# Where the weight buffers, the activation rows and the inner rows begin within 256 bytes

## Time and profile before

| | |
|---|---|
| median of 3 runs | 2599.0 us |
| span of the profiled execution | 2597.1 us |
| TensorE matmuls busy | 99% of the span, 16140 matmuls |
| VectorE busy | 61% |
| ScalarE busy | 46% |
| HBM | 180 GB/s over the span |

### The profile page before, as it was taken

How to read it: one execution, slowest core, us unless ns; L and a number is a source line. 1 busy time by engine, 2 the same in 40 slices (tenths; PEclk the granted TensorE clock), 3 DMA queues, 4 the chain that set the end, 5 groups by cost and what they waited for, 6 DMA issues and landing times.

```text
span 2597.1 us, 41960 instructions
## 1 busy us (share of the span) xinstructions
PE 2574.5 (99%) x16140; PEld 2308.9 (89%) x16140; DVE 1574.0 (61%) x2195; ACT 1188.0 (46%) x1603; POOL 26.8 (1%) x68
## 2 busy tenths in 40 slices
PE   9999999999999999999999999999999999999998
PEld 8999888888888888898999999988999988888886
DVE  5544856556556555565565566666866676666655
ACT  5543445444444344443444454445544444444442
POOL 1000000000000000000000000000000000000000
PEclk9999999999999999999999999999999999999999
DMA  7564555656565666574455566555576656777653
GB/s 250 178 178 130 162 181 178 197 189 194 194 185 184 198 180 194 177 219 140 131 172 169 163 195 191 179 198 163 158 194 177 184 178 196 195 182 188 194 186 122
DMA packets 467827, 468.76 MB, mean 180 GB/s; under 512 B 9294, under 2 KB 384190, under 8 KB 466910
## 3 DMA queue, kind: packets, MB, share of 16 engines
q1 hardware_dynamic: 465648, 459.31, 58.0%
q0 software_dynamic: 2064, 7.82, 0.9%
HBM read 464.93 MB, written 2.10 MB: 180 GB/s over the span
## 4 chain that ended last, share of the span: by engine, by line
PE 93%; DVE 4%; ACT 1%; DMA 1%; issue 1%; SPq 0%; DVEq 0%; ACTq 0%
PE ps L674 16%; PE ps L677 11%; PE ps L678 11%; PE ps L679 11%; PE ps L706 10%; PE ps L708 10%; PE ps L707 10%; PE ps L675 8%; DVE w_lo L2048 1%; DMA raw<-in_w_kv_mem 1%; PE ps L1077 1%; PE ps L1106 0%; PE ps L767 0%; ACT w_hi L1413 0%; PE ps L1113 0%
## 5 line engine op out<-in xcount | busy, mean ns | idle before, releaser
L2048 DVE TENSOR_TENSOR w_lo<-raw,w_hi 128x1024 fp32r<-128x1024 f32 (+1 forms) x876 | 1049.8, 1209 | 784.5 <-ACT w_hi L1413 782.5
L1413 ACT ACTIVATE w_hi<-raw 128x1024 fp32r<-128x1024 f32 (+1 forms) x876 | 904.5, 1045 | 923.1 <-PE ps L708 416.7
L677 PE MATMUL ps<-xa,w_hi 128*128 128x256 f32 (+2 forms) x2304 | 658.9, 286 | 2.0 <-DVE w_lo L2048 2.0
L679 PE MATMUL ps<-xa,w_lo 128*128 128x256 f32 (+2 forms) x2304 | 650.2, 282 | 0.0
L678 PE MATMUL ps<-xa,w_hi 128*128 128x256 f32 (+2 forms) x2304 | 649.8, 282 | 0.0
L674 PE MATMUL ps<-xa,w_hi 128*128 128x512 f32 x1728 | 607.1, 395 | 0.0
L675 PE MATMUL ps<-xa,w_lo 128*128 128x256 f32 x1728 | 483.8, 280 | 0.0
L677 PEld LDWEIGHTS ps<-xa,w_hi 128*128 128x128 f32 x2304 | 436.7, 190 | 12.7 <-issue 9.9
L678 PEld LDWEIGHTS ps<-xa,w_hi 128*128 128x128 f32 x2304 | 434.0, 188 | 1.4 <-issue 1.0
L679 PEld LDWEIGHTS ps<-xa,w_lo 128*128 128x128 f32 x2304 | 433.4, 188 | 0.0
L674 PEld LDWEIGHTS ps<-xa,w_hi 128*128 128x128 f32 x1728 | 324.1, 188 | 78.6
(11 more groups left out here) (354 smaller groups left out, 2525.8 us busy)
## 6 DMA issues: line engine op xcount, KB each, us to landing
raw<-in_mlp_w SPq DMA_DIRECT2D x128, 1024.0 KB
raw<-in_w_in SPq DMA_DIRECT2D x106, 1024.0 KB
raw<-in_w_ffn_in SPq DMA_DIRECT2D x176, 512.0 KB
raw<-in_w_ffn_out SPq DMA_DIRECT2D x40, 1024.0 KB
raw<-in_w_out SPq DMA_DIRECT2D x32, 1024.0 KB
raw<-in_w_o_dsa SPq DMA_DIRECT2D x8, 1024.0 KB
raw<-in_w_o_moba SPq DMA_DIRECT2D x8, 1024.0 KB
raw<-in_w_kv_mem SPq DMA_DIRECT2D x7, 1024.0 KB
```

What stands on the lines that cost most here:

```text
L677: nc.tensor.matmul(o, hi, x_hi, start=opens and ci == 0, stop=False)
L679: ins = nc.tensor.matmul(o, lo, x_hi, start=False, stop=closes and ci == 3)
L1413: return nc.scalar.activation(dst, src, ACT.Copy, **kw)
L2048: V.tensor_tensor(w_lo[:, ps_ % CUT, 0:n], raw[:, bs % RAW, n * half:n * half + n], w_hi[:, ps_ % CUT, 0:n].bitcast(F32), ALU.subtract).th ...
```

## The change

Four sizes are changed. `PAIR` goes from 576 to 548 columns: the chunks of `xa` lie 2192 bytes apart (8 x 256 + 144). A buffer of `w_hi` and `w_lo` is `BUF` = 1036 columns (4144 bytes, 48 past 16 x 256), of which 1024 are used. The chunks of `xh`, `xm` and `xf` are 2064 bytes apart (8 x 256 + 16); `xk` keeps 2048. No instruction is added, removed or moved, and all operands keep their shapes.

```
-PAIR = 576
+PAIR = 548
 EDGE = 4
+SKEW = 4
+BUF = PIECE + 12
...
-        w_hi = sb("w_hi", [P, CUT, PIECE], F32R)
-        w_lo = sb("w_lo", [P, CUT, PIECE], F32R)
+        w_hi = sb("w_hi", [P, CUT, BUF], F32R)
+        w_lo = sb("w_lo", [P, CUT, BUF], F32R)
...
+        def skewed_rows(name, n):
+
+            v = over(name, [P, EDGE + n * (2 * SEQ + SKEW)])
+            return v[:, EDGE:].rearrange("p (c m) -> p c m", c=n)[:, :, 0:2 * SEQ].rearrange("p c (a n) -> p c a n", a=2)
+
         xk = even_rows("xk", DC)
-        xh = even_rows("xh", DC)
-        xm = even_rows("xm", DC)
-        xf = even_rows("xf", FF_CH)
+        xh = skewed_rows("xh", DC)
+        xm = skewed_rows("xm", DC)
+        xf = skewed_rows("xf", FF_CH)
```

## The result

The changed kernel takes 2612.5 us (median of 4 runs, 2611.2 to 2613.3), against 2598.7 us for the kernel before on the same chip (4 runs, 2597.9 to 2599.2): a ratio of 1.0055, 95% interval 1.0043 to 1.0067. The profiled execution has a span of 2609.4 us, 12.3 us above that of before.

What follows compares the result with a forecast made beforehand. TensorE, busy 99% of the span, was taken as the bound through distances between matmul starts. Terms 11.1 + 5.5 + 1.5 - 1.2 = +16.9 us gave a 2614.0 us span, 2615.9 us with 1.9 us added; range 2573 to 2638 us.

Steps and rivals of the forecast that it cites:

- The forecast's own sign of being wrong: Wrong if the wide pair is at or below 351 ns, or if narrow matmuls fall below 117.7 ns.
- Broad from `xh`, `xf`, `xm`: 3036 broad matmuls from the inner rows: 0.5 ns more each, +1.5 us (0 to +13.1).
- Narrow: 6912 narrow matmuls from `xa`: 1.6 ns more each, as `xd` over its twin, +11.1 us (-9.0 to +24.9).
- The bound below: Narrow matmuls: at best 1.3 ns less each, from 117.7 to the 116.4 ns of `xk`.
- Wide: 1728 wide pairs: 1.6 ns more for each of 3456 matmuls, +5.5 us.
- the rival "faster": Moving and stationary reads meet when all begin together; spreading them saves 23.1 us, giving 2575.9 us; chance 0.31.
- Broad from `xa`: 576 broad matmuls at the dearest place: walking gives back half of 4.3 ns, -1.2 us (0 to -2.5).
- The rival "no effect": Distances depend on phase, a state entered after a wait, rather than place; 2599 us, give or take 5; chance 0.16.
- the rule of the Trainium skill: TensorE reads both operands by unshared ports and never waits, so no layout matters; time stays at 2599.0 us.
- The other rule weighed there: Steps of 16, 48 and 144 bytes keep each operand's place within a 16-byte line, so nothing would change.

Runs made afterwards that it cites:

- e1: Kernel before with only the chunks of `xh`, `xm` and `xf` set 16 bytes further each; 2609.7 us against 2598.2, ratio 1.0044.
- e3: Kernel before with `PAIR` 548 and `BUF` 1036, plus 128 bytes behind `w_lo` so that everything further back keeps its place; 2610.8 us, ratio 1.0048.
- e5: Kernel before with `EDGE` 16 instead of 4, putting `xh`, `xm`, `xf`, `xk` at fixed place 32; 2615.8 us, ratio 1.0070.
- e12: Kernel before with `EDGE` 0 instead of 4, putting `xh`, `xm`, `xf`, `xk` at fixed place 224; 2615.8 us, ratio 1.0069.
- e2: Kernel before with only `PAIR` changed, from 576 to 548; 2602.4 us against 2598.2, ratio 1.0017.
- e4: Changed kernel with a gap of 128 bytes between `w_lo` and `xa`, every walk kept; 2612.6 us, ratio 1.0056 to the kernel before.
- e13: Kernel before with `xa` moved by 176 bytes, from place 64 to 240, nothing else moved mod 256; 2590.8 us against 2597.8, ratio 0.9971.
- e9: Kernel before with x_lo of each `xa` chunk 1152 bytes behind x_hi instead of 1088; 2603.8 us, ratio 1.0019.
- e7: Kernel before with `w_lo` beginning at 64 instead of 0, all else kept in place; 2603.0 us, ratio 1.0019.

## Why the prediction was right, and where its sum was not

**Total.** +12.3 us of span against +16.9 forecast: the right sign and nearly the size, but by errors that cancelled, which is luck. The forecast's own sign of being wrong came true: the wide pair was to stay above 351 ns, and it fell to 348.9 ns in the rows and 349.1 ns over the whole trace. That nothing but TensorE's start-to-start distances would move was right, to the cuts' 1209 and 1045 ns.

**Broad from `xh`, `xf`, `xm`: the step that failed.** Taken at +0.5 ns, bounded at +4.3; measured +5.1 on `xh`, and +14.6 us in all instead of +1.5. My argument was that x_hi and x_lo keep one place in common, so the dear case (`xa`) isn't met. What counts is where the stationary operand begins against the moving one. Walking either of them makes these matmuls dear (231.2 ns in e1, 231.4 ns in e3), so does one fixed place, 32 or 224, and in the changed kernel both walk. The upper bound was too low as well: `xa` at 64 was not the dearest place; 224 and 32 cost 6.5 ns more than 240 (e5, e12). The fact that the cheap broad sequence stood at one fixed place I read only as evidence against the rival, not as a thing to lose.

**Narrow.** Taken at +1.6 ns on 6912, +11.1 us; measured +2.5 us, the second term that was mis-sized. The neighbour `xd` over `xa` was a fair twin for 258 columns (118.9 to 120.5 ns in the same stretch, the 1.6 taken; 0.9 over the whole trace) but not for 256, where the dear stretches of the earlier trace rows went away (121.4 to 118.3 ns) while the cheap ones rose by 0.7 ns. The trace of before had both kinds in it, and I priced only the cheap one. The bound below (-1.3 ns, `xk` at 116.4) was mostly rounding: 14 steps between times of two decimals leave 0.7 ns either way, and the exact starts in the trace give 117.1 against 117.4 ns.

**Wide.** Taken at +5.5 us, measured -3.6: the sign was wrong. The pair stands at the 349 ns from which the rival "faster" was to decide, so this rival's gain was real in one form, though no run shows that it comes from reads that no longer meet. Of the -3.6 us, `PAIR` alone gives -0.9 (e2), the buffers another -1.1 (e3), and the last -1.6 go with 128 bytes between the weights and `xa` (e4 against the changed kernel), each from one trace.

**Broad from `xa`.** -1.2 forecast, +0.2 measured: it stays at the price of the dear places.

**The rival "no effect"** was wrong in its result, but its mechanism exists: e13 shows two prices for one set of places. By the rule of the Trainium skill that was weighed there ("SBUF — State Buffer", "Who interferes with whom": TensorE waits for nobody) e5 and e12 would have cost nothing; the runs disagree, with 226.8 against 233.3 ns for one instruction form at five layouts that differ in `EDGE` alone. The other rule weighed there, the 16-byte lines of the same page of the Trainium skill ("Specifications (TRN2)"), fails too: e12 and the kernel before differ by exactly 16 bytes and by 6.5 ns per matmul.

**What stays open.** Which hardware makes the price, and whether it goes by the difference of the two places: no run moves both operands by the same amount. Only five fixed places of the broad form were measured; that the cheap ones are 240 and 0 alone rests on the chunks of e1. Nor is it settled what chooses between the two states at one layout: e13 shows that the dear one can begin behind slotted small matmuls. Of four traces with `xh` at 240 and the weights as before, two have 226.8 and 226.9 ns (before, e9) and two 228.3 and 228.4 ns (e2, e13); both traces with `xh` at 0 are cheap. An experiment on the entry itself wasn't made. Whether a walk costs the plain mean of its places, or more, is open too: the changed kernel's 232.0 ns lies between the fixed places' 226.8 and 233.3.

## What to carry to other kernels

Where TensorE is the bound and its matmuls run back to back, read their start-to-start distance by form and stage, and try fixed beginnings of the two operands mod 256 one at a time: one constant was worth 6.5 ns of 227 here, and two together made the kernel 0.5% faster. Spreading the beginnings was no remedy: it visits the dear places too, and cost 4 to 5 ns on each broad matmul from the inner rows. Take more than one trace of each kernel where a microsecond or two matters. And a form that stands on a cheap place is a thing that a change of layout can lose; price it from the dearest place known, not from its present row.

## What the runs showed of the hardware

- One form (stationary 128x128, moving 128x512, F32R, a load of the stationary operand with each) takes 226.8, 226.9, 232.0, 233.3 and 233.3 ns per start at 2.4 GHz when the stationary operand begins at 240, 0, 80, 32 and 224 and the moving one at 0. The Trainium skill, "TensorE: Matmul & The Clock Gate", "Wait — 56ns, not 53.3ns?", gives columns over clock plus some 2.5 ns, about 215.7 ns for 512 columns. No run here reaches it: the lowest mean of one line of the broad form is 226.5 ns (e7, L708).
- Walking the moving operand's beginning costs as much as walking the stationary one's: 231.4 ns (e3) and 231.2 ns (e1). The price of a matmul isn't set by its own pair of places alone: 226.5 and 231.2 ns for the same pair in e7.
- The same places can have two prices, held over whole stages: 346.7 and 353.3 ns for the wide pair in e13, and 226.8 ns (before) and 228.3 ns (e2) for `xh` at 240.
